# VectorE finishes the next attention unit before it takes the maximum of the unit two ahead, in three attentions

## What is computed

```
s = jnp.where(mask, einsum(q, k) * scale, -inf)     # first: two components c per head, 8 heads
p = jax.nn.softmax(s, axis=-1)
attn = p[:, :, 0] - lam * p[:, :, 1]
out = einsum(attn, v)
...
sc = jnp.where(mask, (qn @ kn + qr @ kr) * scale, min)   # second: 16 heads, 64-wide values
p = jax.nn.softmax(sc, axis=-1);  out = p @ v
...
p = jax.nn.softmax(q @ k * scale, axis=-1);  out = p @ v # third: 4 heads, 256 keys
```

## Time and profile before

| | |
|---|---|
| runs of the kernel before | 3134.01 us median of 3 (3133.16 to 3136.8) |
| the profiled execution | 3135.99 us, span 3134.2 us |
| PE, matmuls | 2625.7 us busy, 84% of the span, 15660 instructions |
| PE, weight loads (beside the matmuls) | 1644.8 us, 52% |
| DVE | 1515.0 us, 48%, 2258 instructions |
| ACT | 936.8 us, 30% |
| chain that ended last | PE 70%, DVE 21%, ACT 4%, issue 3%, DMA 1% |
| granted TensorE clock, mean | 0.871 |
| first, second, third attention | about 1050 to 1227, 2123 to 2420, 2640 to 2688 us |

### The profile page before, as it was taken

How to read it: one execution, slowest core, us unless ns; L and a number is a source line. 1 busy time by engine, 2 the same in 40 slices (tenths; PEclk the granted TensorE clock), 3 DMA queues, 4 the chain that set the end, 5 groups by cost and what they waited for, 6 DMA issues and landing times.

```text
span 3134.2 us, 38075 instructions
## 1 busy us (share of the span) xinstructions
PE 2625.7 (84%) x15660; PEld 1644.8 (52%) x15660; DVE 1515.0 (48%) x2258; ACT 936.8 (30%) x1487; POOL 73.1 (2%) x60
## 2 busy tenths in 40 slices
PE   6969987999979776789997996736775988889997
PEld 4758876888768543334443444513443437434443
DVE  4864327541264444365314553474445254478742
ACT  4322122221212443223222232113444135333321
POOL 0620000000000000000000000000000000000000
PEclk9965588999989766899999996658898999999999
DMA  3100010322312100112222120000001113122221
GB/s 134 68 1 28 28 54 28 108 98 92 108 36 81 54 1 0 54 54 106 87 104 81 67 82 29 1 14 1 29 1 54 69 66 135 33 75 97 83 100 56
DMA packets 27725, 187.99 MB, mean 60 GB/s; under 512 B 3072, under 2 KB 3584, under 8 KB 6048
## 3 DMA queue, kind: packets, MB, share of 16 engines
q1 hardware_dynamic: 27072, 183.77, 16.4%
q10 hardware_dynamic: 480, 1.79, 0.2%
HBM read 183.45 MB, written 2.10 MB: 59 GB/s over the span
## 4 chain that ended last, share of the span: by engine, by line
PE 70%; DVE 21%; ACT 4%; issue 3%; DMA 1%; DVEq 0%; ACTq 0%; POOL 0%; SPq 0%; POOLq 0%
PE ps L428 35%; PE ps L425 19%; DVE wk L522 2%; DVE hn L378 2%; ACT wsp L398 1%; DVE wk L534 1%; PE ps L896 1%; DVE wsp L409 1%; PE ps L1251 1%; DMA raw_w<-slabs 1%; DVE wk L2300 1%; DVE hn L377 1%; DVE wk L1943 1%; PE ps L908 1%; DVE wk L541 1%
## 5 line engine op out<-in xcount | busy, mean ns | idle before, releaser
L428 PE MATMUL ps<-hn,wsp 128*128 128x512 f16 x3120 | 687.7, 383 | 41.3 <-DVE hn L378 34.5
L409 DVE SCALAR_TENSOR_TENSOR wsp<-raw_w,wsp 128x2048 f16<-128x2048 f32 (+1 forms) x176 | 389.4, 2213 | 513.6 <-ACT wsp L398 508.7
L428 PEld LDWEIGHTS ps<-hn,wsp 128*128 128x128 f16 x3120 | 305.0, 99 | 425.6 <-issue 39.5
L428 PE MATMUL ps<-big,wsp 128*128 128x512 f16 (+2 forms) x2304 | 465.4, 364 | 16.5 <-issue 13.7
L425 PE MATMUL ps<-hn,wsp 128*128 128x264 f16 x3552 | 416.9, 281 | 32.2 <-DVE hn L378 32.2
L425 PEld LDWEIGHTS ps<-hn,wsp 128*128 128x128 f16 x3552 | 351.7, 99 | 96.8 <-issue 29.4
L398 ACT ACTIVATE wsp<-raw_w 128x2048 f16<-128x2048 f32 (+1 forms) x176 | 324.7, 1845 | 170.6 <-PE ps L425 68.3
L428 PEld LDWEIGHTS ps<-big,wsp 128*128 128x128 f16 (+1 forms) x2304 | 230.7, 100 | 246.1 <-issue 20.9
L425 PE MATMUL ps<-big,wsp 128*128 128x264 f16 x1920 | 218.4, 277 | 0.0
L425 PEld LDWEIGHTS ps<-big,wsp 128*128 128x128 f16 x1920 | 188.4, 98 | 29.7
L415 ACT ACTIVATE wk<-ps 128x512 f32<-128x512 f32 (+2 forms) x116 | 69.0, 595 | 401.4 <-PE ps L428 400.7
(11 more groups left out here) (338 smaller groups left out, 2701.1 us busy)
## 6 DMA issues: line engine op xcount, KB each, us to landing
raw_w<-slabs SPq DMA_DIRECT2D x166, 1024.0 KB, 5.6
raw_w<-slabs SPq DMA_DIRECT2D x8, 384.0 KB, 5.2
h<-xin SPq DMA_DIRECT2D x1, 2112.0 KB, 8.1
out<-hn SPq DMA_DIRECT2D x8, 256.0 KB, 2.8
big<-memx ACTq DMA_DIRECT2D x1, 1024.0 KB, 4.8
cst<-consts SPq DMA_DIRECT2D x1, 995.5 KB, 9.8
sml<-small SPq DMA_DIRECT2D x1, 768.0 KB, 11.6
wk<-ropes ACTq DMA_DIRECT2D x1, 528.0 KB, 3.6
```

Of the source, the lines that this page charges most:

```text
L409: L.fin(L.eng.scalar_tensor_tensor(wsp[:, n % NW, 1, lo:hi], raw_w[:, q % 2, 0:hi - lo], WSCALE, wsp[:, n % NW, 0, lo:hi], ALU.mult, ALU.s ...
L428: return L.eng.matmul(ps[:rows, b, 0:T], lhsT, rhs, start=start, stop=stop)
```

## The change

In the three loops of VectorE the two calls are exchanged: `l1_mix(n + 1)` or `unit_norm(n + 1)` comes first, `l1_max(n + 2)` or `unit_max(n + 2)` second. The code before the loops is as it was: max(0), max(1), mix(0).

```
@@ second attention
                 if i == 1 and hd + 1 < 16:
                     head_dve(hd + 1)
+                if n + 1 < 64:
+                    unit_norm(n + 1, ((n + 1) % 4 + 1) * P)
                 if n + 2 < 64:
                     unit_max(n + 2, ((n + 2) % 4 + 1) * P, sq_, acc_next())
-                if n + 1 < 64:
-                    unit_norm(n + 1, ((n + 1) % 4 + 1) * P)
@@ third attention
             for n in range(64, 80):
+                if n + 1 < 80:
+                    unit_norm(n + 1, MEM)
                 if n + 2 < 80:
                     unit_max(n + 2, MEM, 1.0 / 16, acc_next())
-                if n + 1 < 80:
-                    unit_norm(n + 1, MEM)
@@ first attention
             for n in range(32):
+                if n + 1 < 32:
+                    l1_mix(n + 1)
                 if n + 2 < 32:
                     l1_max(n + 2)
-                if n + 1 < 32:
-                    l1_mix(n + 1)
```

## The result

| | before | after |
|---|---|---|
| median | 3135.41 us of 4 runs (3133.16 to 3137.83) | 3110.18 us of 4 (3104.33 to 3112.21) |
| after over before, 95% interval | | 0.9916 (0.9901 to 0.993) |
| profiled execution | 3135.99 us, span 3134.2 | 3104.33 us, span 3102.6 |
| mean granted clock | 0.871 | 0.866 |

A forecast was written before the change was run, and what follows sets the result against it. No engine was full; a ring of waits between PE and DVE set the pace. Gains of 17.3 + 20.4 + 3.6 = 41.3 us, taken off the median of 3134.01, gave 3093 us; range 3070 to 3113.

The forecast's parts named there:

- a ring: First attention: scores(n+1), max(n+1), mix(n), turn(n), scores(n+2) wait on each other; ceiling of the order's gain there 41.3 us.
- the own range of the forecast: Whole kernel: 3080 to 3106 us around 3093, single terms off by a third; chance 0.78.
- rival 2: Second attention: a head's end gains nothing, the next head's start being held by late exp(384) or ACT; 3113 us, chance 0.08.
- the signs that it had named for being wrong: ACT's waits for DVE grow and PE's values wait long for ACT, or a stretch's granted clock moves by over 0.1.
- 2.31 us for a head at today's clock: First attention: gains of 0.65, 0.96, 0.70 and 0 us for units with 272, 400, 528 and 144 keys.
- The three units that were to gain: First attention: units with 272, 400 and 528 keys, whose meta transpose would start 0.65, 0.96 and 0.70 us earlier.
- 17.3 us for the stage: First attention: 2.31 us a head over 8 heads, 18.5, less the first and last unit; bounds 0 and 41.3.
- Rival 1: First attention: a denser PE is granted 2.4 GHz for longer, 23 us more gain, 3070 us; chance 0.10.
- 1.36 us a passage: Second attention: at each of 15 passages to a next head, the 256-key turn starts 1.36 us earlier; 20.4 us in all.
- Rival 3: All three attentions: late exps reach PE through out, turn and values, up to 90 us, 3183 us; chance 0.04.
- 2.41 us a unit: Third attention: the longest ring, through ACT, takes 4.81 us for two units; gain 0.26 a unit, 14 times, 3.6 us.
- What is late next is ACT's string max, exp, out: After the exchange, out(n) and turn(n+1) queue on ACT behind a later exp(n+2); each stage's gain was taken by this string.

## Why the prediction was right, and where it fell short

The sign, the range and the mechanism of the order held: the mix and the norm had stood in a ring behind a maximum by the order of the list alone. That 3110 lies in the range is in part luck. It missed the own range of the forecast, to which it had given 0.78, and lies where the range had been stretched for rival 2, which is not what happened. And of the signs that it had named for being wrong, both came: the clock of a stretch moved by over 0.1, and ACT's waits for DVE grew while L908 waited for ACT. Going by the prediction's own steps:

- *First attention, 2.31 us for a head at today's clock.* 2.40 measured at the lower clock, 2.45 at a mixed one. The three units that were to gain did, each within 0.04 us of its term, and L1267 waits for L1737 with 272 and 400 keys as said; L2300 waits less (43.5 us, before 74.6).
- *17.3 us for the stage, "I keep scores and max in place".* **This is the step that failed.** It kept not only their places but the clock they ran at, and the clock went from 0.64 to 0.50. At equal clock 2.40 times 7.5 heads would be 18.0; 5.8 came. The 12 us between went to heads that had run partly at 2.4 GHz. The head of 18.20 us at 0.69 in the run with the later start, and the products behind the change, with 145.2 us at 0.75, show that it was the clock.
- *Rival 1, the clock follows upward, 0.10.* Wrong in sign here. The Trainium skill, page "Perfetto Trace Analysis", matmul optimizations, has the engine's power scale with its utilization. This case's traces don't bear it out as a rule: PE's busy share rose from 129.05 of 174.08 us to 150.16 of 168.29, and the clock fell to 0.50. (A part of that busy time is the slow clock's own doing; but the same 554 matmuls also came in 5.8 us less.) The clock moved by 0.14, downward.
- *Second attention, 1.36 us a passage.* Mis-sized: 0.93 for a plain one, 0.98 over all. The exp of 512 keys starts late as forecast, and the values come 1.71 us behind it (2185.73 to 2187.44), where the reckoning had put them at 1.73 (2200.37 + 0.65 to 2202.22 + 0.53). What it left out is PE's own start. A turn that follows values at once begins 0.17 us after them (2188.24, 2190.65, 2191.97), three in a row on the path: 0.51 a head. Before, these turns waited 0.39, 0.21 and 1.37 us for DVE, and the sum took all of that waiting as slack. That three of 0.17 make up the missing 0.43 is worked out from rows; no run took them away, and the removed waits show only that these are not their cause. The wait that was to go has gone: L896 waited 44.3 us besides the split of head 15 and waits 12.4 now.
- *Rival 3, ACT's late exps reach PE.* Its mechanism is there, L908's 30.3 us of waiting for ACT, and ACT's own waits for the maximum grew, L1722's in the first attention from 48.9 to 56.9 us and L1432's in the second from 71.6 to 83.4; yet no stage got longer, let alone by the 48 us from which it would decide. The Trainium skill, page "TensorE: Matmul & The Clock Gate", on engine queue depths, lets an instruction of ACT wait for all that is queued ahead. The trace agrees as to the order (L1737 at 1098.83 stands behind both exps) and says nothing for the full price.
- *Rival 2, the head's end gives nothing.* It does give; the next head's start was not held.
- *Third attention, 2.41 us a unit.* 2.38. The stage gave 5.4 against 3.6, but not by the order alone: the clock there went from 0.91 to 0.96, and in the kernel with this part alone, at 0.87, the same stage gave 2.3. That it came out above the forecast is the clock's luck.
- *"What is late next is ACT's string max, exp, out".* Right, and the copy between the exps shows it: 17 us behind the change, 1.50 us a head of it at equal clock, and nothing in the old order.

**What stays open** is why the clock of the first attention goes where it goes. It follows neither more nor less work for TensorE (heads among the first five of each stage; a first head is some 0.1 us shorter than a later one at the same clock):

| kernel | head wholly at the lower clock | granted clock of the stage |
|---|---|---|
| before | 22.77 us | 0.64 |
| before, products | 23.9 | 0.51 |
| before, two pauses | 24.1 | 0.54 |
| before, copy between | first head only, 22.66 | 0.70 |
| after | 20.37 | 0.50 |
| after, one pause | 21.03 | 0.61 |
| after, products | none seen | 0.75 |
| after, copy between | first head only, 18.78 | 0.67 |
| after, copy between and products | none seen | 0.82 |

The same order in the first attention gives about the same clock in different kernels (0.50 in the change, in the first part alone and without the guarding waits, 0.52 with a later start; in the old order 0.64, 0.68 and 0.64). Whether the length of the head, its inner timing or something else decides, no run here separates; the length of a head is in part the clock's own doing, so that the table alone can't tell cause from effect. Also untried is moving L1267's wait for the output copy from the meta transpose to the values, which would take ACT's string off the path without moving the copy. The two share a PSUM bank, and the kernel's wait keeps them apart.

## What to carry to other kernels

Where two engines hand work round in a ring, look for what stands in it by list order alone: a step whose input has long been ready, queued behind one that waits. Putting it first gains at most its length on every turn of the ring, and how much of it comes is set by what is late next. Where the stretch runs at a mixed clock, price such a gain at both levels, and give the case in which the clock falls a chance as well as that in which it rises.

## What the runs showed of the hardware

- A head of the first attention with less idle time for TensorE got the lower clock throughout (0.64 to 0.50), and with 5 us of added DVE work, spread over 8 heads, it was 0.61 and the profiled stage 3.4 us shorter, which the total does not show. In the old order it was 0.54 with 10.4 us of such work, and the stage 21 us longer.
- A head of the first attention in the new order took 20.37 us wholly at 1.2 GHz and 18.20 with 2.4 GHz for 7 us of it; in the old order 22.77 and 20.65.
- 48 small products in 16 units changed the clock from 0.50 to 0.75 behind the change (23 us less) and from 0.64 to 0.51 in the old order (21 us more).
- A weight load of a turn that follows values with nothing to wait for starts 0.17 to 0.3 us after them (9.7 us in 48 loads). With one of the two met waits before it taken out it is the same (9.6 in 47).
